# A fused two-model transformer forward pass on one core: inverse root-mean-square columns made by GpSimd with a power of -0.5

## The reference

```
h = rmsnorm(x, norm_pre[l, 0]) * (1.0 + sc1) + sh1
y = swiglu(h, ffn_w_gate[l, 0], ffn_w_up[l, 0], ffn_w_down[l, 0])
x = x + 0.5 * g1 * rmsnorm(y, norm_post[l, 0])
h = rmsnorm(x, norm_pre[l, 1]) * (1.0 + sc2) + sh2
y = hybrid_mixer(h, ...)
x = x + g2 * rmsnorm(y, norm_post[l, 1])
h = rmsnorm(x, norm_pre[l, 2]) * (1.0 + sc3) + sh3
y = swiglu(h, ffn_w_gate[l, 1], ffn_w_up[l, 1], ffn_w_down[l, 1])
x = x + 0.5 * g3 * rmsnorm(y, norm_post[l, 2])
```

```
def rmsnorm(x, g):
    xf = x.astype(jnp.float32)
    y = xf * lax.rsqrt(jnp.mean(xf * xf, axis=-1, keepdims=True) + EPS)
    return (y * g.astype(jnp.float32)).astype(x.dtype)
```

## Time and profile before

| | |
|---|---|
| median of three runs | 3181.19 us (3179.1 to 3194.51) |
| profiled execution | 3182.83 us |
| its span | 3181.0 us |
| PE busy | 3090.9 us, 97%, 19928 instructions |
| DVE busy | 2255.9 us, 71%, 4134 instructions |
| ACT busy | 1637.7 us, 51%, 3094 instructions |
| POOL busy | 692.7 us, 22%, 692 instructions |
| chain that ended last | PE 86%; DVE 8%; DMA 2%; DVEq 2%; ACT 2% |

### The profile page before, as it was taken

The page is one execution under the profiler, slowest core; times in us unless marked ns, Lnnn a source line. Parts: engine busy times, 40 slices in busy tenths (PEclk is TensorE's granted clock), DMA queues, the critical chain, the costliest instruction groups (busy, mean ns, idle before and its releaser), DMA issues.

```text
span 3181.0 us, 58397 instructions
## 1 busy us (share of the span) xinstructions
PE 3090.9 (97%) x19928; PEld 2753.1 (87%) x19928; DVE 2255.9 (71%) x4134; ACT 1637.7 (51%) x3094; POOL 692.7 (22%) x692
## 2 busy tenths in 40 slices
PE   6999999999999999999999999999999999999999
PEld 5779999988888876899999788879987998988898
DVE  6649988877777435798888677777666777766654
ACT  1225578864444354355888444455455545445543
POOL 0107845520000110285555000000100010010000
PEclk9999999999999998999999999999999999999999
DMA  7635555558887431455444788877854787884354
GB/s 284 240 134 167 187 165 173 163 204 264 262 259 253 130 120 40 136 184 170 139 138 133 251 263 262 261 248 260 264 197 141 248 262 257 276 260 144 123 183 152
DMA packets 178000, 635.86 MB, mean 200 GB/s; under 512 B 23976, under 2 KB 23984, under 8 KB 177232
## 3 DMA queue, kind: packets, MB, share of 16 engines
q1 hardware_dynamic: 134560, 491.48, 46.9%
q0 software_dynamic: 43296, 142.77, 13.5%
q10 hardware_dynamic: 16, 0.01, 0.0%
HBM read 630.88 MB, written 9.53 MB: 201 GB/s over the span
## 4 chain that ended last, share of the span: by engine, by line
PE 86%; DVE 8%; DMA 2%; DVEq 2%; ACT 2%; issue 1%; SPq 0%; ACTq 0%
PE ps L773 21%; PE ps L597 12%; PE ps L599 11%; PE ps L598 11%; PE ps L755 7%; PE ps L585 6%; PE ps L632 2%; PE ps L1167 2%; PE ps L1166 2%; PE ps L1035 1%; DMA ring<-stream 1%; PE ps L968 1%; PE ps L873 1%; PE ps L701 1%; PE ps L660 1%
## 5 line engine op out<-in xcount | busy, mean ns | idle before, releaser
L1781 DVE TENSOR_TENSOR unit_low<-ring,unit_high 128x1024 fp32r<-128x1024 f32 x480 | 638.8, 1331 | 172.3 <-ACT unit_high L1267 163.8
L1267 ACT CAST unit_high<-ring 128x1024 fp32r<-128x1024 f32 x524 | 548.2, 1047 | 230.6 <-PE ps L599 167.3
L599 PE MATMUL ps<-expert_x_high,unit_low 128*128 128x256 f32 x1968 | 556.1, 283 | 0.0
L597 PE MATMUL ps<-expert_x_high,unit_high 128*128 128x256 f32 x1552 | 447.9, 289 | 2.0 <-DVE unit_low L1781 1.8
L598 PE MATMUL ps<-expert_x_low,unit_high 128*128 128x256 f32 x1552 | 433.8, 280 | 0.0
L599 PEld LDWEIGHTS ps<-expert_x_high,unit_low 128*128 128x128 f32 x1968 | 370.5, 188 | 0.0
L773 PE MATMUL ps<-unit_low,expert_high 128*128 128x512 f32 x1016 | 325.1, 401 | 2.4 <-DVE unit_low L1781 2.4
L773 PE MATMUL ps<-unit_high,expert_high 128*128 128x512 f32 x1016 | 317.6, 393 | 4.6 <-ACT unit_high L1267 4.4
L773 PE MATMUL ps<-unit_high,expert_low 128*128 128x512 f32 x1016 | 320.1, 395 | 0.1
L597 PEld LDWEIGHTS ps<-expert_x_high,unit_high 128*128 128x128 f32 x1552 | 294.2, 190 | 6.5 <-issue 2.6
L598 PEld LDWEIGHTS ps<-expert_x_low,unit_high 128*128 128x128 f32 x1552 | 293.3, 189 | 0.0
(11 more groups left out here) (388 smaller groups left out, 7054.6 us busy)
## 6 DMA issues: line engine op xcount, KB each, us to landing
ring<-stream SPq DMA_DIRECT2D x754, 512.0 KB, 4.1
arena<-stream SPq DMA_DIRECT2D x160, 512.0 KB, 4.3
score<-ada POOLq DMA_DIRECT2D x128, 512.0 KB, 5.1
arena<-ada POOLq DMA_DIRECT2D x96, 512.0 KB, 5.1
arena<-bias_tiles POOLq DMA_DIRECT2D x48, 192.0 KB, 2.7
arena<-ada SPq DMA_DIRECT2D x8, 1024.0 KB, 17.3
bias_tiles<-bias_rows POOLq DMA_DIRECT2D x8, 768.0 KB, 14.9
arena<-gate_home POOLq DMA_DIRECT2D x7, 512.0 KB, 10.3
```

The costliest lines, as they stand in the source:

```text
L597: pe.matmul(out, hi[:, kt, :], xh[:, kt, :], start=(kt == 0), stop=False)
L599: mm = pe.matmul(out, lo[:, kt, :], xh[:, kt, :], start=False, stop=(kt == KD - 1))
L1267: nc.scalar.copy(hi, raw_of(unit)).then_inc(whi_ready, 1)
L1781: V.tensor_tensor(out=lo, in0=raw_of(unit), in1=hi, op=ALU.subtract).then_inc(wlo_ready, 1)
```

## The change

The roots on ScalarE and the reciprocals on VectorE at the late boundaries are gone. GpSimd takes both sums' mean with EPS (first piece's share from `halved` as before, second piece's with a tensor_scalar), drains, and raises the mean to the power -0.5 with a tensor_tensor against a constant column. The signals that announced a root now announce an inverse. The calls stand at the end of each phase in GpSimd's stream, y's two halves and then x's two, so ahead of the DMAs of the next phase.

```
@@ scalar
-            def x_rooted_of(ph, tt):
-                no = PHASES.index(ph) - 3
-                act.drain()
-                act.wait_ge(x_halved, TT * no + tt + 1)
-                nc.scalar.activation(x_root[:, tt:tt + 1], x_sum[:, 2 * tt + 1:2 * tt + 2], ACT.Sqrt,
-                                     bias=x_half[:, tt:tt + 1], scale=1.0 / D).then_inc(x_rooted, 1)
...
-                def y_rooted_of(tt):
-                    act.drain()
-                    act.wait_ge(y_halved, TT * no + tt + 1)
-                    nc.scalar.activation(y_root[:, tt:tt + 1], y_sum[:, 2 * tt + 1:2 * tt + 2], ACT.Sqrt,
-                                         bias=y_half[:, tt:tt + 1], scale=1.0 / D).then_inc(y_rooted, 1)
...
@@ vector, x_scaled_of
                 dve.wait_ge(x_rooted, TT * no + tt + 1)
-                V.reciprocal(x_inv[:, tt:tt + 1], x_root[:, tt:tt + 1])
-                dve.drain()
                 V.tensor_scalar(stat[:, tt, 0:P], ident, x_inv[:, tt:tt + 1], None, ALU.mult).then_inc(x_scaled, 1)
@@ vector, y_scale
                     dve.wait_ge(y_rooted, TT * no + tt + 1)
-                    V.reciprocal(y_inv[:, tt:tt + 1], y_root[:, tt:tt + 1])
                     dve.drain()
@@ vector, setup
             V.memset(eps, EPS)
+            V.memset(small[:, 31:32], -0.5)
@@ gpsimd
+            def inverse_root(inv, mean, sums, half, squared, halved, signal):
+                pool.wait_ge(*squared)
+                pool.wait_ge(*halved)
+                G.tensor_scalar(mean, sums, 1.0 / D, half, ALU.mult, ALU.add)
+                pool.drain()
+                G.tensor_tensor(out=inv, in0=mean, in1=small[:, 31:32], op=ALU.pow).then_inc(signal, 1)
+
+            def y_inverse(ph, tt):
+                no = PHASES.index(ph) - 4
+                inverse_root(y_inv[:, tt:tt + 1], y_root[:, tt:tt + 1], y_sum[:, 2 * tt + 1:2 * tt + 2], y_half[:, tt:tt + 1],
+                             (y_squared, 4 * no + 2 * tt + 2), (y_halved, TT * no + tt + 1), y_rooted)
...
@@ gpsimd, behind each phase
+                if late_phase(ph):
+                    y_inverse(ph, 0)
+                    y_inverse(ph, 1)
+                if PHASES.index(ph) >= 3 and ph != phases[-1]:
+                    x_inverse(ph, 0)
+                    x_inverse(ph, 1)
```

More of the change, by code:

```diff
@@ L1333, in y_square @@
                     nc.scalar.activation(junk[:, k, :], y, ACT.Square, accum_out=y_sum[:, k:k + 1]).then_inc(y_squared, 1)
-                def y_rooted_of(tt):
-                    act.drain()
-                    act.wait_ge(y_halved, TT * no + tt + 1)
-                    nc.scalar.activation(y_root[:, tt:tt + 1], y_sum[:, 2 * tt + 1:2 * tt + 2], ACT.Sqrt,
-                                         bias=y_half[:, tt:tt + 1], scale=1.0 / D).then_inc(y_rooted, 1)
                 y_square(0)
                 y_square(1)
-                y_rooted_of(0)
                 y_square(2)
@@ L1348, in norm_out @@
                 y_square(3)
-                y_rooted_of(1)
                 if more:
                     x_square(ph, 1)
-                    x_rooted_of(ph, 0)
                     x_square(ph, 2)
                     x_square(ph, 3)
-                    x_rooted_of(ph, 1)
             def next_high(ph, unit_last):
@@ L2613, in _, with x_inverse @@
             G = nc.gpsimd
+            def inverse_root(inv, mean, sums, half, squared, halved, signal):
[8 more added lines that the diff above has]
+                             (y_squared, 4 * no + 2 * tt + 2), (y_halved, TT * no + tt + 1), y_rooted)
+            def x_inverse(ph, tt):
+                no = PHASES.index(ph) - 3
+                inverse_root(x_inv[:, tt:tt + 1], x_root[:, tt:tt + 1], x_sum[:, 2 * tt + 1:2 * tt + 2], x_half[:, tt:tt + 1],
+                             (x_squared, 4 * no + 2 * tt + 2), (x_halved, TT * no + tt + 1), x_rooted)
             def low(unit, n):
```

## The result

The changed kernel took 3205.49 us (median of 4 runs, 3202.13 to 3210.26) where the kernel before took 3180.14 (4 runs): a ratio of 1.0067, 95% interval 1.0042 to 1.0092. That is some 21 us slower. The prediction said 3183.5, with a range of 3177 to 3202, so the median lies 3.5 us outside it. The ratio put on the 3181.19 us that the forecast starts from gives 3202.5 (3194.6 to 3210.5), at the edge of the range. The forecast was 2.3 us slower, and the case that the result came nearest to in size is rival C, of which the mechanism did not happen.

A forecast was written before the change was run, and what follows sets the result against it. TensorE, busy 97%, was taken to bound the kernel, with 13.2 us of waits within the change's reach. 3 x 0.15 + 6 x 0.3 + 0 = +2.3 us on the 3181.19 median gave 3183.5 us, range 3177 to 3202.

The forecast's parts named there:

- rival C: GpSimd's power is a slow routine, 2.06 us per inverse, four in a row at a boundary: about 3210 us; chance 0.16.
- drain 0.19: Drain between tensor_scalar and power on GpSimd, priced 0.19 us from a drain behind four tiny memsets.
- The power, taken at 0.40: Power on 128x1 in each GpSimd inverse, priced 0.40 us by the longest of GpSimd's small copies.
- y, second half: change 0: Behind ffn0, inverse ready at 2327.78, the addition that needs it started at 2327.80: no change.
- The first half likewise, with VectorE busy in front of it: Inverse of y's first half at a boundary: hidden behind VectorE's work, change 0.
- port 0.3 us at each of six: GpSimd's x first half against VectorE's addition, up to 0.75 us late or nothing; 0.3 us each, 1.8 us in all.
- 0.15 exposed at the quick boundaries: Scaling of x's second half 0.28 us later, half exposed: 0.15 us at three quick boundaries, 0 at three slow ones.
- The end, 0: Behind ffn3, inverse ready at 3176.48 before the addition starts at 3176.53: change 0.
- GpSimd's queue behind the last power, 0: Next phase's DMAs after peer1 issued about 1.3 us later, first used by VectorE 20 us on: hidden.
- Rival A: Power is cheap, 0.52 to 0.7 us per inverse, so boundaries and end gain: -2.6 us, 3178.6; chance 0.18.
- Rival B: GpSimd loses the port to VectorE's addition at every boundary, 0.75 us each: +5 us, 3186; chance 0.15.
- Rival D: Change fully hidden in TensorE's spare matmuls: no difference, 3181; counted as part of the forecast's own range.

The follow-up runs named there:

- late_ladder: Kernel before, with one GpSimd drain behind each late boundary's wait for squares and more drains inside peer1, ffn0 and ffn1: 3219.34 us.
- early_drain: Changed kernel with one more GpSimd drain at each late boundary, behind the phase's last DMA and ahead of the waits for the squares: 3189.46 us, ratio 1.0033.
- after_filled: Changed kernel with longer rows of spare matmuls at the six boundaries, to fill TensorE's wait for the scaled identity: 3193.77 us, ratio 1.0043.
- before_filled: Kernel before, with 15 more spare matmuls behind each hyb and 10 more behind ffn1: 3173.2 us, ratio 0.9969.
- by_semaphore: Changed kernel with the inverse's drain replaced by a semaphore between tensor_scalar and power: 3184.65 us, ratio 1.0006.
- semaphore_filled: Changed kernel with a semaphore for the inverse's drain, and 18 more spare matmuls behind each hyb, 12 behind ffn1, 2 behind ffn0 and ffn2: 3180.98 us, ratio 0.9999.
- before_filled2: Second timing of the kernel before with 15 more spare matmuls behind each hyb and 10 more behind ffn1: 3172.32 us, ratio 0.9989.

## Why the prediction was wrong

The step that failed is "drain 0.19", a term of the 0.92 us per inverse. It was priced by the one drain in the trace, at 0.3 us of the program, when GpSimd had issued no DMA yet. On the path GpSimd stood behind 2 to 162 of them. The prediction did look at GpSimd's queue, but only at the DMAs behind the last power; those ahead of the first one have no term in it, and they had indeed long landed. As late_ladder shows, landed is not settled. With 0.082 us for each, 36, 17, 34, 36 and 16 DMAs and peer1's 4.8 us make 16.2 us. early_drain, which takes just this out, ends 17.0 us earlier, but the two sums are not made of the same things and their nearness is in part chance: its six boundaries are 18.8 us shorter, 13.7 of it TensorE's waits (32.3 to 18.6; the rest of the drains had been covered) and 5.1 the turnings at a higher clock behind shorter waits, while its phases took 1.8 us more.

The sum as measured, from the first boundary to the end, is +25.4. TensorE's waits are +19.1 of it: 13.7 for the drains, some 3.9 for y's inverses and x's first half (with the short drains), and 1.6 because peer1's wait was the long one of its two values in early_drain (whether it was under the changed kernel's drain can't be told). From first to second turning it is +7.7. With every wait filled the changed kernel's six distances are 16.8 us (after_filled) and those of the kernel before 15.4 (before_filled): 1.4 is x's second half, and the other 6.3 is the clock, 11.4 lost to it after and 5.1 before. The end has +0.4, the phases between -1.9. The prediction gave the clock nothing; only rival C had a term for it.

What is left without the long drains is what the prediction had tried to work out, with +2.3. By place:

- The power, taken at 0.40: 0.55 us. The tensor_scalar, 0.21: 0.26. From tensor_scalar to power, 0.21 + 0.19 = 0.40: 0.41 with the drain, 0.34 with the semaphore. From the end of the read-out of x's second square to the scaling it is 1.09 (2335.91 to 2337.00) in place of 0.92 (0.64 before). The kind of row was well chosen, the size a little low. The bound from above, 2.06, came nowhere near.
- "y, second half: change 0": 0.16 late, because 1.10 from the square is more than the 0.94 that VectorE gave. "The first half likewise, with VectorE busy in front of it": wrong. VectorE's gate product itself waits for ScalarE (0.53 us at 2323.93 before), so only its own 0.69 us cover the inverse, and it is 0.25 late. Together 0.4 us, at four of five boundaries.
- x's first half, "port 0.3 us at each of six": 0.3 us at each of five (behind peer1 no power met an addition). The mechanism was right, the size luck: the 0.3 stood for a chance between 0.75 and nothing, and there is no race. The power begins inside VectorE's addition each time, takes 0.85 us (0.91 with the semaphore) where it takes 0.55 alone, and ends 0.41 us behind the addition's end. The rule in the Trainium skill, "SBUF — State Buffer", section "Who interferes with whom", is that a VectorE instruction with two SBUF inputs and a GpSimd instruction that reads SBUF shut each other out. The trace agrees with it here, and in early_drain: behind ffn1 a power that begins 0.08 us behind such a subtraction (2660.26 to 2661.47) takes 1.56 and ends 0.43 behind its end. No run moved the addition away; the cause rests on these rows. What the prediction missed is that y's first inverse meets such a subtraction too, behind the hybs and ffn1:

```profile
2659.94 0.26 POOL L2596 TENSOR_SCALAR tok<-tok 128x1 f32<-128x1 f32 x1 [16.83 <-DVE tok L1799]
2660.34 1.56 POOL L2598 TENSOR_TENSOR tok<-tok,small 128x1 f32<-128x1 f32 x1
```

- x's second half, 0.15 exposed at the quick boundaries: from first to second turning it was 2.56 us before and is 2.80 in early_drain and 2.74 in by_semaphore: 0.24 and 0.18. At the three slow ones it was taken as hidden; with the waits filled it shows there too (2.80 in after_filled against 2.56 in before_filled). Right in kind, too small at three places and missing at three.
- The end, 0: +0.44. The last addition does find its inverse ready, as said; it is y's first half that comes late there (3191.74 to 3193.07 from gate product to addition, where it was 0.84), 0.25 of it without the drain's two DMAs.
- GpSimd's queue behind the last power, 0: right; no phase grew by over 0.5 us.

By the semaphore kernel, that is 1.7 (y) + 1.7 (x's first half, peer1's 0.2 in it) + 1.1 (x's second) + 0.3 (the end) = 4.8 us, and 4.7 is what lies between semaphore_filled and before_filled2. early_drain and by_semaphore lie 8.4 and 8.1 us above the kernel before. What goes beyond 4.8 is not the inverses' own: 1.6 is peer1's wait, over 1 the clock behind somewhat longer waits, and in early_drain 0.6 more for the drains that stand where the semaphore is.

Rival A (cheap power) did not come. Rival B's port was lost at five of six boundaries, at 0.3 and not 0.75: the power begins only 0.44 us before the addition's end (2333.31, and 2333.00 + 0.75). Rival C gave 3210 for a power of 2.06 us and a fourfold chain. Its signs were named rightly (waits over 3 us at all six boundaries, quick stages at a lower clock), but one of them, powers of over 1 us, fails, and the number is right by accident. Its term for the clock, +4, was the right mechanism; it measured 6.3. Rival D (fully hidden) did not come either; by_semaphore's timing says "no difference", while its trace says +8. What remains open is why peer1's wait has two values, why the hyb phases differ by up to 3 us between kernels that are alike there, why a drain pays by the number of DMAs, and where that price ends.

## What to carry to other kernels

Before an engine that has only issued DMAs gets a step on the critical path, count the DMAs since its last drain: a drain there is not the drain of another place in the same trace. Order two dependent instructions on it by a semaphore, or put one drain into its idle time beforehand. And where TensorE stands for some 3 us or more at a boundary, as at three of the kernel before, look at the granted clock behind it: spare matmuls that fill the wait cost nothing in these traces and give back 1.4 to 2.3 us each time, 5.1 in sum, more than the change's best case (rival A, 2.6 us).

## What the runs showed of the hardware

- A drain of GpSimd right behind a DMA that it issued waits for the landing: 5.2 us behind one block of 512 KB that lands in 5.1, ending 0.07 us behind the landing; behind 8 and 16 blocks 0.36 and 0.69.
- Long after the landing it still takes 0.04 us + 0.082 us for each DMA issued since the last drain (2 to 50 DMAs, seven drains, 8 to 38 us behind the last landing); with 162 it took 4.8.
- A power of 128x1 on GpSimd takes 0.55 us, a tensor_scalar of 128x1 0.26; beside a VectorE instruction with two SBUF inputs they took up to 1.6 and 1.24, and a semaphore between the two is 0.07 us shorter than a drain with nothing to settle.
- TensorE's 16 records of turning took 2.05 us behind standstills of 0.4 to 2.6 us, 2.5 to 3.7 behind 2.8 to 3.4, and 3.4 to 3.8 behind 4.2 to 6.3, at a granted clock down to 0.50; with the same wait filled by matmuls they took 2.05 again, at 1.00.
